# Attention output projections of a hybrid trunk taken in pieces around the last value products

## What is computed

```python
y = jnp.concatenate([y_a, y_b, y_c], axis=-1) @ w_out[l]
x = x + rms_norm(y, norm_mix_post[l])
h = rms_norm(x, norm_x_pre[l])
y = memory_cross_attention(h, rms_norm(mem, norm_mem[l]), x_w_q[l], x_w_kv[l], x_w_o[l])
x = x + rms_norm(y, norm_x_post[l])
```

## Time and profile before

| | |
|---|---|
| median of 3 runs | 1696.82 us (1694.28 to 1698.57) |
| profiled execution, its time | 1691.17 us |
| its span | 1689.3 us |
| TensorE (matmul) busy | 1595.3 us |
| VectorE, ScalarE busy | 911.9 us, 733.1 us |
| mean granted TensorE clock | 0.991 |
| instructions | 19237 |

### The profile page before, as it was taken

How to read it: one execution, slowest core, us unless ns; L and a number is a source line. 1 busy time by engine, 2 the same in 40 slices (tenths; PEclk the granted TensorE clock), 3 DMA queues, 4 the chain that set the end, 5 groups by cost and what they waited for, 6 DMA issues and landing times.

```text
span 1689.3 us, 19237 instructions
## 1 busy us (share of the span) xinstructions
PE 1595.3 (94%) x7372; PEld 1241.1 (73%) x7372; DVE 911.9 (54%) x1418; ACT 733.1 (43%) x1246; POOL 1.3 (0%) x6
## 2 busy tenths in 40 slices
PE   6999989999999999999989989898999999999996
PEld 5775558876768888888767655687767888888884
DVE  5766644855365555532287666458354755555223
ACT  5534654534344444432245355455254444444221
POOL 0000000000000000000000000000000000000000
PEclk9999999999999999999999999999999999999998
DMA  6320013440212333333213200225303133333321
GB/s 227 113 75 25 1 50 101 150 125 25 88 50 87 100 100 101 100 111 100 87 51 97 78 13 1 86 89 162 113 13 100 40 101 101 102 103 102 104 73 50
DMA packets 38539, 143.48 MB, mean 85 GB/s; under 512 B 4272, under 2 KB 4400, under 8 KB 37936
## 3 DMA queue, kind: packets, MB, share of 16 engines
q1 hardware_dynamic: 38448, 142.25, 26.5%
HBM read 140.13 MB, written 2.10 MB: 84 GB/s over the span
## 4 chain that ended last, share of the span: by engine, by line
PE 86%; DVE 7%; ACT 4%; issue 3%; DMA 0%; SPq 0%; DVEq 0%; ACTq 0%
PE bank L526 25%; PE bank L528 24%; PE bank L527 24%; PE bank L776 2%; PE bank L861 2%; PE bank L804 2%; PE bank L851 1%; PE bank L792 1%; PE bank L718 1%; DVE x L1367 1%; DVE tn_x L1332 1%; PE bank L707 1%; PE bank L573 1%; DVE acc L1273 1%; DVE h_lo L1337 1%
## 5 line engine op out<-in xcount | busy, mean ns | idle before, releaser
L526 PE MATMUL bank<-h_hi,w_hi 128*128 128x512 f32 x1312 | 522.4, 398 | 35.3 <-DVE h_lo L1279 16.5
L1292 DVE TENSOR_TENSOR w_lo<-raw,w_hi 128x1024 fp32r<-128x1024 f32 x254 | 310.3, 1225 | 431.3 <-ACT w_hi L921 429.1
L528 PE MATMUL bank<-h_hi,w_lo 128*128 128x512 f32 x1312 | 513.6, 391 | 0.0
L527 PE MATMUL bank<-h_lo,w_hi 128*128 128x512 f32 x1312 | 513.4, 391 | 0.0
L921 ACT ACTIVATE w_hi<-raw 128x1024 fp32r<-128x1024 f32 x254 | 265.9, 1050 | 189.1 <-PE bank L528 178.5
L526 PEld LDWEIGHTS bank<-h_hi,w_hi 128*128 128x128 f32 x1312 | 247.9, 189 | 103.8 <-issue 23.2
L527 PEld LDWEIGHTS bank<-h_lo,w_hi 128*128 128x128 f32 x1312 | 248.4, 189 | 53.1 <-issue 2.4
L528 PEld LDWEIGHTS bank<-h_hi,w_lo 128*128 128x128 f32 x1312 | 248.0, 189 | 52.3
L527 PE MATMUL bank<-a_lo,w_hi 128*128 128x512 f32 x352 | 136.9, 389 | 0.0
L526 PE MATMUL bank<-a_hi,w_hi 128*128 128x512 f32 x352 | 136.9, 389 | 0.0
L528 PE MATMUL bank<-a_hi,w_lo 128*128 128x512 f32 x352 | 136.9, 389 | 0.0
(11 more groups left out here) (208 smaller groups left out, 1856.4 us busy)
## 6 DMA issues: line engine op xcount, KB each, us to landing
raw<-w_in SPq DMA_DIRECT2D x254, 512.0 KB, 3.6
x<-x_in SPq DMA_DIRECT2D x4, 512.0 KB, 8.1
mem<-mem_in SPq DMA_DIRECT2D x2, 1024.0 KB, 4.9
out<-x SPq DMA_DIRECT2D x4, 512.0 KB, 2.6
consts<-c_in SPq DMA_DIRECT2D x1, 1600.0 KB, 13.1
mem_sq<-mem_in SPq DMA_DIRECT2D x1, 1024.0 KB, 5.9
gains<-g_in SPq DMA_DIRECT2D x1, 80.0 KB, 3.6
```

The source lines that it names most:

```text
L526: pe.matmul(out_ap, l_hi, r_hi, start=start, stop=False)
L527: pe.matmul(out_ap, l_hi, r_lo, start=False, stop=False)
L528: return pe.matmul(out_ap, l_lo, r_hi, start=False, stop=stop)
L1292: dve.tensor_tensor(w_lo[:, s, :], raw[:, s, :], w_hi[:, s, :].bitcast(F32), ALU.subtract)\
```

## The change

The first two output tiles of each of the two output projections are issued in pieces. In the mixing projection the steps take the feature tiles in the order 4, 5, 0, 1, 2, 3, 6, 7. Six steps of tile 0 are issued ahead of the last pair's `pair_out`, one step of tile 0 and seven of tile 1 behind it, then the last step of each, then tiles 2 to 7 whole. The waits for `out_lo` stand ahead of the single steps. In the cross-attention projection six steps of tile 0 go ahead of the last head's `x_out`, six of tile 1 behind it, then the last two of tile 0 and of tile 1, then the others, with a wait ahead of every step. The weight stream keeps its bytes. Only the columns read from a unit of `out` are taken in another order.

```diff
+OUT_ORDER = (4, 5, 0, 1, 2, 3, 6, 7)
+EARLY = 2
...
-    def whole(name, u0, n, engine="act"):
+    def whole(name, u0, n, engine="act", order=range(KT)):
         for m in range(n):
-            add(name, [(u0 + m, k * P) for k in range(KT)], engine)
+            add(name, [(u0 + m, k * P) for k in order], engine)
...
-    whole("out", U_OUT, KT)
+    whole("out", U_OUT, KT, order=OUT_ORDER)
...
-                    def attention(a, heads, probs, klen, emit_scores, emit_out):
+                    def attention(a, heads, probs, klen, emit_scores, emit_out, before_last):
...
                             w = u - LAG - OUT_LAG
+                            if w == n_units - 1:
+                                before_last()
                             if w >= 0 and w % TB == TB - 1:
...
+                    def out_step(m, j):
+
+                        if m == 0 and j == 0:
+                            pe.wait_ge(ml_lo, count(ml_lo, layer, ML_PAIRS))
+                        if OUT_ORDER[j] not in (4, 5):
+                            pe.wait_ge(mix_at["out_lo"], count(mix_at["out_lo"], layer, j - 1))
+                        project_step("out", m, j, lambda j: h_hi[:, OUT_ORDER[j], :], lambda j: h_lo[:, OUT_ORDER[j], :])
+
                     for s in range(PAIR_STEPS + PAIR_LAG + 1):
                         if s < PAIR_STEPS:
                             pair_scores(s)
                         t = s - PAIR_LAG
+                        if t == PAIR_STEPS:
+                            for j in range(KT - 2):
+                                out_step(0, j)
                         if t >= 1 and t % TB == 0:
                             pair_out(t // TB - 1)
...
-                    pe.wait_ge(mix_at["out_lo"], count(mix_at["out_lo"], layer, MIX_PAIRS))
-                    pe.wait_ge(ml_lo, count(ml_lo, layer, ML_PAIRS))
-                    for m in range(KT):
-                        project("out", m, tiles(h_hi), tiles(h_lo))
+                    out_step(0, KT - 2)
+                    for j in range(KT - 1):
+                        out_step(1, j)
+                    for m in range(EARLY):
+                        out_step(m, KT - 1)
+                    for m in range(EARLY, KT):
+                        for j in range(KT):
+                            out_step(m, j)
...
-                    attention(x_at, X_HEADS, p_x, lambda qb: N_MEM, x_scores, x_out)
-                    pe.wait_ge(x_at["out_lo"], count(x_at["out_lo"], layer, KT))
-                    for m in range(KT):
-                        project("xo", m, tiles(h_hi), tiles(h_lo))
+                    def xo_step(m, k):
+
+                        pe.wait_ge(x_at["out_lo"], count(x_at["out_lo"], layer, k + 1))
+                        project_step("xo", m, k, tiles(h_hi), tiles(h_lo))
+
+                    def xo_first():
+
+                        for k in range(KT - 2):
+                            xo_step(0, k)
+
+                    attention(x_at, X_HEADS, p_x, lambda qb: N_MEM, x_scores, x_out, xo_first)
+                    for k in range(KT - 2):
+                        xo_step(1, k)
+                    for m in range(EARLY):
+                        for k in range(KT - 2, KT):
+                            xo_step(m, k)
+                    for m in range(EARLY, KT):
+                        for k in range(KT):
+                            xo_step(m, k)
```

## The result

The change made the kernel faster by more than I had forecast: 1678.20 us (four runs, 1676.93 to 1680.11) against 1696.55 (four runs, 1694.28 to 1698.57). The ratio is 0.9898, 95% interval 0.9884 to 0.9912. Measured a second time, the ratio was 0.9896 (0.9881 to 0.9911), 17.5 us by the medians.

What follows compares the result with a forecast made beforehand. TensorE was taken to bound the kernel; 3.15 + 4.52 for mixing and 2 x 2.27 for cross-attention give 12.2 us, so 1679.0 for the profiled execution and 1684.6 for the median, range 1680 to 1690.5.

Steps and rivals of the forecast that it cites:

- What bounds the kernel: TensorE carries 86% of the chain; four waits at the two output projections, in both layers, total 12.2 us.
- first and second hole: Mixing: idle TensorE before the last value products (0.91 us) and before the projection (2.93), both filled by projection steps.
- Layer 0 of mixing, 3.15 us: Layer 0's mixing projection: 0.91 + 2.93 from idle times, 0.11 for a burst not restarted, less 0.80 at tile 2.
- The wait at the third tile: Mixing projection: tile 2 waits 0.69 us for tile 0's bank and restarts a burst (0.11), a loss of 0.80.
- Cross-attention, 2.27 us a layer: Cross-attention and its output projection: 0.80 + 1.48 + 0.11 - 0.12 us gained in each layer.
- Queues moved past: Load of mem starts 3.17 us later, delaying VectorE and tile 1's eviction; tile 3 keeps 0.8 us spare, no cost.
- Added waits: Both output projections: 220 more waits in all, taken to cost nothing, bounded by 0.11 us each.
- The clock, 1.37 us: Layer 1's mixing projection: half-clock stretch behind the 2.9 us idle time goes, 1.37 us won; bounds nothing and 2.74.
- I take the same amount off it: Median of the runs assumed to stay 5.65 us above the profiled execution, turning 1679.0 into 1684.6.
- The signs that I had named: Profile after: low-part waits and gaps gone, about 0.7 us at the third mixing tile, layer 1 clock 1.00, w_lo stalls unchanged.
- The first, that the clock falls elsewhere: Low clock stays in layer 1 (1686.0 us) or comes at each of four places (1690.1 us); chance 0.13.
- Rivals 2 to 4: Gain returns as weight waits, 1692.3 us (0.06); waits break the stream, 1708.8 (0.03); steps put ahead wait, 1688 (0.05).

Runs made afterwards that it cites:

- the padded holes: Kernel before the change, with unread matmuls in the first and second mixing holes and the second cross-attention hole, no step moved: 1689.15 us, ratio 0.9967.
- single paddings: Kernel before the change, unread matmuls in only the first mixing hole, only the second, or only the cross-attention one: ratios 0.9995, 0.9987, 1.0012.

## Why the prediction was wrong

**What bounds the kernel, and the first and second hole: right.** All four waits are gone, and nothing came back elsewhere: memory keys and values and the feed-forward part kept their lengths within 0.04 us.

**Layer 0 of mixing, 3.15 us: measured 3.01,** and 3.04 in layer 1 without its fall. The wait at the third tile was there. The 0.59 of its row counts from the modelled end of the last matmul; from start to start the wait is 0.75 us and the burst 0.11, 0.86 in place of 0.80. The Trainium skill's sentence (TensorE: Matmul & The Clock Gate, Loop structure matters more than you think) that the next tile's matmuls follow the copy at once did not hold for this order of steps. With tile 0 finished sooner, tile 2 had no wait.

**Cross-attention, 2.27 us a layer: measured 2.54 and 2.58.** I had measured the holes from the modelled end of the last matmul. A matmul in a stream would have started before that end. From start to start the first hole gave 0.90 us in place of 0.80, the second with its burst 1.86 in place of 1.59, and tile 2 lost 0.20 in place of 0.12.

**Queues moved past: right.** Mem was issued 2.7 us later than before (249.47 against 246.76, in an execution that came to this point 0.5 us sooner, so 3.2 as forecast), VectorE waited for it, and tile 3 did not. **Added waits: right,** nothing.

**The clock, 1.37 us: the step that failed,** together with the sentence "I take the same amount off it". I sized the term from the one execution that I had: one fall in layer 1, with a bound of two. The median execution of before has a mean clock of 0.988 where the profiled one had 0.991, and after the change it is 0.992 to 0.993. Over the whole span the clock gave about 6.5 us in place of 1.37, by the clocks of the second comparison: 11.2 + 6.5 = 17.7, where 17.5 was measured there and 18.4 in the first. Without the clock the prediction's sum comes to 10.8, against the 11.2 read from the parts, so the holes were right. I had seen that the profiled execution was 5.65 us faster than the median and had carried that distance over unchanged. But it was just this distance that the change removed (after, the profiled execution is 1.0 us below the median). Two further falls of the profile itself, ahead of the feed-forward part of either layer, I did not connect with the change at all. In the first profile after both were gone, in the second one of them was back. The mechanism was right where I had it: the second hole brings a fall behind it. But it does so in 10 of 12 layers and not in one of two, the first hole keeps the clock low once it has fallen, and there are falls ahead of the feed-forward part. The signs that I had named all came true to within hundredths of a us. They looked at the holes, and none at the mean clock of the runs.

**Rivals.** The first, that the clock falls elsewhere, named the right quantity with the wrong sign. The Trainium skill's sentence (TensorE: Matmul & The Clock Gate, A second HAM failure mode: psum-queue depth-cycling) that short idle times between groups can make the clock swing agrees with the padded holes and with the falls behind the second hole, for the holes removed and not for the new wait at tile 2, behind which no fall was seen in either profile. Rivals 2 to 4 fell: w_lo's waits stayed at 11.6 us, the waits cost nothing, and the steps put ahead did not wait.

**What stays open.** Why a fall comes in one execution and not in the next of the same kernel, what brings those ahead of the first mixing hole and ahead of the feed-forward part, and why single paddings gave -0.3, -2.6 and +1.9 us where all three together gave -6.0. Whether the places of the falls depend on each other, or on a shift of the work in time, no run tests. The falls make most of the spread of this kernel's times, but not all: of the 5.4 us between its two profiles 1.3 lie at the start, at full clock.

## What to carry to other kernels

Work that is ready belongs into a wait of TensorE even where the wait is a microsecond wide: it wins the width, and here more than half as much again (6.5 us beside 11.2) through the clock. Where a kernel's runs scatter, compare their mean clocks before sizing anything, and ask of which kind the profiled one is. An excess of the median over the profiled run is not a constant to be carried over, it may be what the change removes. Where two output tiles are opened at once, finish the first of them an eviction's length before the second.

## What had not been expected of the hardware

The mean granted clock and the time go together so closely that they sort 67 runs of one kernel on three chips into four groups, 1.44 us to a thousandth. A fall costs very different amounts by its place: 1.37 us at the start of the projection, 2.2 us in the value products alone (4.54 against 2.37), and nothing that shows in the norms between the layers, where the first profile after had a mean clock of 0.86 from 838 to 850 us and the part from 834.33 to 862.53 took 28.20 us, as before. Six microseconds were gained by matmuls whose result nobody reads. With 2.9 us of idle time ahead of the projection a fall stood at or just behind its end in 10 of 12 layers. And a clock that had already fallen stayed low through an idle time of 0.9 us in five layers of five, where with TensorE busy in that place it was back by then in five of five.
